# Query projections moved between the row products of a hybrid decoder kernel

## What is computed

```
qb = rmsnorm(h @ W_q), kb = rmsnorm(h @ W_k)          # 8 heads, forgetting attention (branch B)
# branch C: matrix memory, 4 heads, per head and chunk
dmat  = b_t - b_s + i_s  (s <= t)
m_t   = max(max_s dmat, b + m)
num   = (exp(dmat - m_t) * (q k^T)) @ v + exp(b + m - m_t) * C q
den   = the same with ones in place of v, and n in place of C
h     = num / max(|den|, exp(-m_t))
C_new = decay * C + sum_s w_s v_s k_s^T               # of the prompt and of each sample
```

## Time and profile before

| quantity | value |
|---|---|
| median of three runs | 3294.8 us (3291.88 to 3295.17) |
| the profiled execution | 3302.38 us, span 3300.7 us |
| PE busy | 3135.0 us, 95% of the span |
| DVE, ACT busy | 1154.3 us (35%), 818.5 us (25%) |
| mean granted TensorE clock | 0.97 |
| memory stage, from the transposes to the vb projection, layer 1 | 663.33 to 805.34 us |
| the same, layer 2 | 2298.47 to 2437.31 us |

### The profile page before, as it was taken

The page is one execution under the profiler, slowest core; times in us unless marked ns, Lnnn a source line. Parts: engine busy times, 40 slices in busy tenths (PEclk is TensorE's granted clock), DMA queues, the critical chain, the costliest instruction groups (busy, mean ns, idle before and its releaser), DMA issues.

```text
span 3300.7 us, 54135 instructions
## 1 busy us (share of the span) xinstructions
PE 3135.0 (95%) x23518; PEld 2799.6 (85%) x23518; DVE 1154.3 (35%) x1933; ACT 818.5 (25%) x1213; POOL 138.5 (4%) x269
## 2 busy tenths in 40 slices
PE   6999999989999998999989999999899999899998
PEld 4999997857677898999989999887576778899998
DVE  3333334234432234332343323332444223343333
ACT  3221224222331122211222212242223212222121
POOL 0000000000311000000000000000003120000000
PEclk9999999988999999999999999999899999999999
DMA  5444431101248432342223443312012583322212
GB/s 237 147 167 165 154 134 68 65 26 60 76 152 267 138 135 77 122 159 103 90 77 128 160 173 144 126 53 90 26 47 88 179 270 105 127 77 84 96 68 76
DMA packets 117725, 390.82 MB, mean 118 GB/s; under 512 B 12672, under 2 KB 63200, under 8 KB 99184
## 3 DMA queue, kind: packets, MB, share of 16 engines
q1 hardware_dynamic: 99456, 338.36, 29.0%
q0 software_dynamic: 14432, 34.09, 3.0%
q10 hardware_dynamic: 3600, 14.91, 1.1%
HBM read 373.62 MB, written 13.69 MB: 117 GB/s over the span
## 4 chain that ended last, share of the span: by engine, by line
PE 84%; DMA 6%; DVE 5%; ACT 3%; issue 1%; SPq 1%; ACTq 0%; DVEq 0%
PE g L838 74%; PE tb L838 5%; PE q L838 5%; DMA w<-in_w_up 3%; DMA area<-in_w_ada 1%; ACT area L1723 1%; DMA area<-in_cache_v 1%; DVE w_lo L1923 1%; DVE area L2127 1%; SPq L703 1%; ACT area L1729 0%; ACT w_hi L1460 0%; DMA area<-in_cache_k 0%; DVE w_rest L1881 0%; DVE acts_lo L1942 0%
## 5 line engine op out<-in xcount | busy, mean ns | idle before, releaser
L838 PE MATMUL g<-h_hi,w_hi 128*128 128x272 f32 x2784 | 584.4, 291 | 28.8 <-DVE h_lo L1867 12.4
L1460 ACT ACTIVATE w_hi<-w 128x1024 fp32r<-128x1024 f32 (+2 forms) x232 | 266.2, 1147 | 1271.5 <-PE g L838 930.5
L838 PE MATMUL g<-h_hi,w_lo 128*128 128x272 f32 x2784 | 579.1, 289 | 0.0
L838 PE MATMUL g<-h_lo,w_hi 128*128 128x272 f32 x2784 | 575.9, 288 | 0.0
L1923 DVE TENSOR_TENSOR w_lo<-w,w_hi 128x1024 fp32r<-128x1024 f32 (+2 forms) x232 | 309.8, 1335 | 527.1 <-ACT w_hi L1460 523.9
L838 PEld LDWEIGHTS g<-h_hi,w_hi 128*128 128x128 f32 x2784 | 440.5, 190 | 48.2 <-ACT area L1469 33.8
L838 PEld LDWEIGHTS g<-h_lo,w_hi 128*128 128x128 f32 x2784 | 439.0, 189 | 0.0
L838 PEld LDWEIGHTS g<-h_hi,w_lo 128*128 128x128 f32 x2784 | 438.2, 189 | 0.0
L838 PE MATMUL g<-h_hi,w_rest 128*128 128x272 f32 x1184 | 344.0, 293 | 0.0
L838 PE MATMUL g<-acts_hi,w_hi 128*128 128x272 f32 x1408 | 294.8, 290 | 0.0
L838 PE MATMUL g<-acts_hi,w_lo 128*128 128x272 f32 x1408 | 291.2, 288 | 0.0
(11 more groups left out here) (296 smaller groups left out, 4142.8 us busy)
## 6 DMA issues: line engine op xcount, KB each, us to landing
w<-in_w_up SPq DMA_DIRECT2D x44, 2048.0 KB, 8.1
w<-in_w_ada SPq DMA_DIRECT2D x32, 2048.0 KB, 8.2
w<-in_w_in SPq DMA_DIRECT2D x16, 2048.0 KB, 8.3
w<-in_w_down SPq DMA_DIRECT2D x16, 1536.0 KB, 7.2
w<-in_w_gate SPq DMA_DIRECT2D x48, 512.0 KB, 5.7
w<-in_w_down SPq DMA_DIRECT2D x16, 1280.0 KB, 5.7
area<-in_cache_k SPq DMA_DIRECT2D x72, 256.0 KB, 4.1
area<-in_cache_v SPq DMA_DIRECT2D x72, 256.0 KB, 4.6
```

Of the source, the lines that this page charges most:

```text
L838: return pe.matmul(o, a, b, start=start, stop=stop, skip_group_check=True, **kw)
L1460: ac.activation(WH[i % 2][:, 0:n], W[place][:, o:o + n], ACT.Copy).then_inc(s_wh, 1)
```

## The change

The schedule gets four ticks ahead of the heads: six blocks behind each of the four row products. The 16 steps of the heads hold 4 blocks (12 steps) and 5 (the last four) in place of 5 each, the five ticks of the tail 8, 8, 8, 6, 6 in place of 12, 12, 8, 8, 8. All later ticks are renumbered by HEADS_AT = 4. ScalarE and VectorE get the reads and splits that belong to the new ticks, ScalarE between its GB copies, VectorE ahead of the copy of the sample rows.

```
-IN_MLSTM = Schedule(0, FILL_A, [5] * 16 + [12, 12, 8, 8, 8])
+ROWS_AT, HEADS_AT = 0, HC
+IN_MLSTM = Schedule(0, FILL_A, [6] * HC + [4] * 12 + [5] * 4 + [8, 8, 8, 6, 6])
 ...
                 for h in range(HC):
                     product(unit(), [sel_neg[:, HB + h, :]], lambda k: ROWG[0:ROWS, :])
+                    fill(l, IN_MLSTM, ROWS_AT + h)
 ...
-                each(4, lambda i, p: ac.activation(halves(GB[:, i, :]), both(p), ACT.Copy))
+                for h in range(HC):
+                    read(l, IN_MLSTM.early[ROWS_AT + h])
+                    p = mine()
+                    drained(ac.activation(halves(GB[:, h, :]), both(p), ACT.Copy), p)
+                    read(l, IN_MLSTM.late[ROWS_AT + h])
 ...
                 un.take(4)
+                for h in range(HC):
+                    lo_fills(l, IN_MLSTM.early[ROWS_AT + h] + IN_MLSTM.late[ROWS_AT + h])
```

In the two state products of the samples, the order of the four products changes, and the wait for the spread v of both heads stands ahead of the first:

```
                     p = unit()
-                    for h2 in range(2):
-                        wait(t["vblk"])
-                        h = 2 * hp + h2
-                        for sh in range(2):
+                    wait(t["vblk"], 2)
+                    for sh in range(2):
+                        for h2 in range(2):
+                            h = 2 * hp + h2
                             last = mm(G[64 * h2:64 * h2 + 64, 2 * p + sh, :], KCT[0:NS, TILES, h * 64:(h + 1) * 64],
                                       VBLK[0:NS, h2, 4 * sh:4 * sh + 4, :], True, True)
```

More of the change, by code:

```diff
@@ L1145, in _ @@
                             qk(n + 1)
-                        fill(l, IN_MLSTM, n)
+                        fill(l, IN_MLSTM, HEADS_AT + n)
                         weigh(n)
@@ L1168, in _ @@
                 last.then_inc(s_sintra, 1)
-                fill(l, IN_MLSTM, 16)
+                fill(l, IN_MLSTM, HEADS_AT + 16)
                 wait(t["sw"])
@@ L1183, in _ @@
                 last.then_inc(s_num, 1)
-                fill(l, IN_MLSTM, 17)
+                fill(l, IN_MLSTM, HEADS_AT + 17)
                 wait(t["kws"])
@@ L1194, in _ @@
                     last.then_inc(s_unit, 1)
-                    fill(l, IN_MLSTM, 18 + hp)
+                    fill(l, IN_MLSTM, HEADS_AT + 18 + hp)
                 p = unit()
@@ L1200, in _ @@
                 last.then_inc(s_unit, 1)
-                fill(l, IN_MLSTM, 20)
+                fill(l, IN_MLSTM, HEADS_AT + 20)
                 project_tokens(l, "vb", sums=True)
@@ L1634, in _ @@
                         n = h * TILES + j
-                        read(l, IN_MLSTM.early[n])
+                        read(l, IN_MLSTM.early[HEADS_AT + n])
                         a = COL[:, j * 12 + HB + h:j * 12 + HB + h + 1]
@@ L1644, in _ @@
                         last.then_inc(s_e, 1)
-                        read(l, IN_MLSTM.late[n])
+                        read(l, IN_MLSTM.late[HEADS_AT + n])
                     un.take()
@@ L1649, in _ @@
                 un.take()
-                read(l, IN_MLSTM.early[16] + IN_MLSTM.late[16])
+                read(l, IN_MLSTM.early[HEADS_AT + 16] + IN_MLSTM.late[HEADS_AT + 16])
                 wait(t["stn"])
@@ L1660, in _ @@
                 last.then_inc(s_ses, 1)
-                read(l, IN_MLSTM.early[17] + IN_MLSTM.late[17])
+                read(l, IN_MLSTM.early[HEADS_AT + 17] + IN_MLSTM.late[HEADS_AT + 17])
                 ac.wait_ge(s_outa, outs.value())
@@ L1664, in _ @@
                     un.take()
-                    read(l, IN_MLSTM.early[18 + hp] + IN_MLSTM.late[18 + hp])
+                    read(l, IN_MLSTM.early[HEADS_AT + 18 + hp] + IN_MLSTM.late[HEADS_AT + 18 + hp])
                     if hp == 1:
@@ L1670, in _ @@
                 un.take()
-                read(l, IN_MLSTM.early[20] + IN_MLSTM.late[20])
+                read(l, IN_MLSTM.early[HEADS_AT + 20] + IN_MLSTM.late[HEADS_AT + 20])
                 wait(t["stn"])
@@ L1674, in _ @@
                 wait(t["yc"])
-                read(l, IN_MLSTM.early[21] + IN_MLSTM.late[21])
+                read(l, IN_MLSTM.early[HEADS_AT + 21] + IN_MLSTM.late[HEADS_AT + 21])
                 ac.wait_ge(s_outa, outs.value())
@@ L2115, in _ @@
                             diag(n + 1)
-                        lo_fills(l, IN_MLSTM.early[n])
+                        lo_fills(l, IN_MLSTM.early[HEADS_AT + n])
                         wait(t["e"])
@@ L2120, in _ @@
                                          ALU.mult).then_inc(s_wt, 1)
-                        lo_fills(l, IN_MLSTM.late[n])
+                        lo_fills(l, IN_MLSTM.late[HEADS_AT + n])
                     p = mine()
@@ L2135, in _ @@
                 ve.sem_inc(s_stn, 1)
-                lo_fills(l, IN_MLSTM.early[16] + IN_MLSTM.late[16])
+                lo_fills(l, IN_MLSTM.early[HEADS_AT + 16] + IN_MLSTM.late[HEADS_AT + 16])
                 ve.tensor_tensor(ARG[0:NS], GB[0:NS, :, NP:T], seq_later[:, None, :].to_broadcast([NS, HC, NS]),
@@ L2157, in _ @@
                 last.then_inc(s_sw, 1)
-                lo_fills(l, IN_MLSTM.early[17] + IN_MLSTM.late[17])
+                lo_fills(l, IN_MLSTM.early[HEADS_AT + 17] + IN_MLSTM.late[HEADS_AT + 17])
                 wait(t["num"])
@@ L2175, in _ @@
                     p = mine()
-                    lo_fills(l, IN_MLSTM.early[18 + hp] + IN_MLSTM.late[18 + hp])
+                    lo_fills(l, IN_MLSTM.early[HEADS_AT + 18 + hp] + IN_MLSTM.late[HEADS_AT + 18 + hp])
                     ve.tensor_tensor(CS[:, hp].rearrange("p (a s) v -> p a (s v)", a=2),
@@ L2187, in _ @@
                 ve.sem_inc(s_stn, 1)
-                lo_fills(l, IN_MLSTM.early[20] + IN_MLSTM.late[20] + IN_MLSTM.early[21])
+                lo_fills(l, IN_MLSTM.early[HEADS_AT + 20] + IN_MLSTM.late[HEADS_AT + 20] + IN_MLSTM.early[HEADS_AT + 21])
                 lo_part(l, *[("vb", i) for i in range(4)], ("merge", 0))
```

## The result

| kernel | median, runs | ratio to before, 95% |
|---|---|---|
| before | 3294.99 us (3291.88 to 3298.64), 4 | |
| after | 3316.74 us (3315.91 to 3317.99), 4 | 1.0068 [1.0053, 1.0083] |

The change costs 21.7 us. The forecast of 3299 us had the sign but a fifth of the size, and the range ended at 3309: the prediction was wrong. The profiled execution took 3317.99 us (span 3316.3).

A forecast was written before the change was run, and what follows sets the result against it. TensorE bounds the kernel, carrying 84% of the chain of waits. Row stage 5.1, heads -2.9, tail 0 give 2.2 us per layer, 4.4 in both: 3302.4 to 3306.8 us profiled, 3299 us as median, range 3290 to 3309.

The forecast's parts named there:

- the sign: Whole kernel: the change makes it slower, by 2.2 us per layer, 4.4 in both.
- row stage, work and wait, less the 15.86 of before: Row stage: 17.3 us of work at full clock, 0.9 for switches and 0.8 of added wait, against 15.86 now.
- row stage, clock: Row stage: blocks bring the clock back within a tick or two; 4 us at the lower clock, 2.0 lost.
- heads, blocks and ends: Heads: blocks save 3.4 and 0.3 us, first end 1.1 longer, third 0.3 shorter; -2.9 us per layer.
- heads, clock: Heads: lower-clock stretches after each boundary (0.73 and 0.88) left as they are, so no change.
- tail: Tail: twelve blocks less, but new waits; taken as 0, between -2.1 and +1.6 us per layer.
- The range of none to 6: Row stage: ends of the clock loss, none to 6 us, around the 2.0 taken.
- the three ends: Heads, last weighing to next head's first: 10.2 us at the first boundary, 8.9 at the others.
- the two added waits: TensorE waits 0.8 us at the first weighing and idles some 2.7 us for a weight block's rest in the tail.
- the alternation at nothing: State products: alternating two heads costs nothing, as two already run at a time; 1.9 us as before.
- The first rival: Row stage: row products hold the clock down, 4 us more per layer, num another 1.6; 3310 us, chance 0.33.
- The second, heads that get warmer: Heads: blocks leave them warmer, one 4.4 us stretch goes per layer, all else at low end; 3282 us, chance 0.13.

The follow-up runs named there:

- e3: Kernel after with 28 products nobody reads added ahead of the wait for the rows, before the row stage; 3311.51 us, ratio 1.0054.
- e4: Kernel after with 36 products nobody reads added at each of the three ends of heads, ahead of the next head's first blocks; 3287.61 us, ratio 0.9982.
- e6: Kernel before with 36 products nobody reads added at each of the same three ends of heads; 3277.30 us, ratio 0.9953.
- e12: Kernel after with five blocks for six behind each row product, the four left over in the tail's first tick; 3289.52 us, ratio 0.9978.
- e2: Kernel after with the state products in their old order, so the schedule change alone; 3313.89 us, ratio 1.0062.
- e8: Kernel after with one block moved from the tail to the heads' last step; 3303.91 us, ratio 1.0036.
- e5: Kernel after with unread products added: 28 ahead of the rows, 36 at each of three ends of heads, 24 in the tail; 3283.90 us, ratio 0.9967.
- e7: Kernel before with unread products added: 28 ahead of the rows and 36 at each of three ends of heads; 3273.71 us, ratio 0.9939.
- e9: Kernel before with another table: heads 5, 5, 5, 5, then three times 12, 4, 4, 4 blocks, tail 12, 8, 8, 4, 4; 3258.47 us, ratio 0.9887.

## Why the prediction was wrong, by its steps

| step, per layer | forecast | layer 1, 2 | what the runs show |
|---|---|---|---|
| row stage, work and wait, less the 15.86 of before | +3.1 | +4.5 | 20.35 at clock 1.00 (e3), 19.0 forecast |
| row stage, clock | +2.0 | +2.5, +5.5 | the stage less 20.35 |
| heads, blocks and ends | -2.9 | -2.1 | e4 against e6 at clock 1.00 |
| heads, clock | 0 | +2.1, +4.1 | low clock's cost after less before |
| tail | 0 | +0.3, +1.8 | its upper end, 1.6, with num at 6.83 us |
| sum | +2.2 | +7.3, +13.8 | |

**The step that failed** is the sentence on the heads: "the stretches at the lower clock after each boundary (clock 0.73 and 0.88) I leave as they are." I had forecast the ends to the tenth of a microsecond, the first one 1.1 us longer, and had read what stands behind an end in rows 5, and did not join the two. Those stretches were worth 8 to 10 us per layer before anything was changed, the largest thing to be won in the stage, and they grew by 3.1 us on average, more than the 2.1 us that the blocks gave: 6.2 of the 16.6 us that the forecast's sum missed in both layers. What it lacked was the link from the idle time to the clock behind it, which e4, e6 and e12 show.

**The clock of the row stage** was the second miss: 4.0 us on average for 2.0. One execution gives this value only roughly: the four kernels that have this stage with the idle ahead left alone (after, e2, e4, e8) show eight of them, from 21.88 to 25.82 us, 23.5 on average, a loss of 3.2. With the idle filled (e3, e5) the four stages take 20.35 to 20.92. My reason, blocks from 1.3 us on bring the clock back, is true, but the start differs: the same stage with the same 3.46 us of idle ahead ran at 0.88 and 0.77 in the two layers, and that of e12, with four blocks less, at 0.63 in layer 1. The range of none to 6 held these; the value did not.

**The work of the row stage** was 1.4 us short. I took half of a row product's 1.81 us for full clock. In e5, whose stage in layer 1 is at 1.00, a tick with its row product takes 3.54 us, from one product's start to the next:

```profile
662.08 1.16 PE L839 MATMUL g<-area,cst 12*128 12x272 f32 x4
...
665.62 1.18 PE L839 MATMUL g<-area,cst 12*128 12x272 f32 x4
```

With six blocks at 0.376 (2.26) that leaves 1.28 us for the product and both switches, for my 0.91 and 0.1 to 0.2: four times 0.2 to 0.3. The 0.91 was right (in e7 a row product at full clock starts at 659.91 and the next at 660.83), so the switches cost more than I gave them. The sample rows with the first head's row product took 1.56 us in the kernel after (678.49 to 680.05) for my 1.2.

**Right** were the sign, the three ends, the two added waits (the four terms of the first one add up to 4.2 us, not 4.1), the alternation at nothing, and that the tail gives nothing for its twelve blocks. The first rival (3310 us) was on the side on which the result fell. Its condition, 8 us at the lower clock in the row stage, was met in layer 2 (0.77 over 25.82 us is 12 us) and not in layer 1 (0.88 over 22.83 us is 5.5 us), but its mechanism is not borne out for the changed stage: with the idle ahead filled, the same row products between the ticks left the clock up (e3, e5). The second, heads that get warmer, had it the wrong way round here, though the mechanism is real: e12, four blocks away, is 27 us faster than the kernel after.

**Open** stays what sets how long the lower clock lasts at the start of the row stage from one layer, kernel and execution to the next (with the same idle ahead, 0.77 to 0.92 over the stage in after, e2, e4 and e8), and how the tail of e9 divides.

## What to carry to other kernels

Price an idle time of the engine that bounds the kernel twice: once as it is, and once by the lower clock of the stretch that follows it, read from the stretch behind every such gap; in e12 the second part was twice the first. Work that can be moved belongs first into the gaps that it can close (an end of a head holds twelve blocks), not into a stage where the engine never waits. And where a table deals out work in periods, see whether its period puts a helper's long operation ahead of the one wait that counts each time: five blocks for six behind each of four products, with the four left over in the tail, moved 27 us.

## What the runs showed that I had not expected

- Work without use pays: 36 products in each of three ends, 4.3 us each, made the kernel after 29 us faster and the one before 16.4 us.
- The length of the idle alone does not tell the clock behind it: after 4.26 us the next stretch ran at 0.88 before the change, after 4.25 us at 0.72 in the kernel after.
- Row products of 12 rows in a run let the clock fall 2.0 and 5.0 us into the stage even when TensorE was busy up to its start (e7), while the same products with blocks between them kept 1.00 through all four ticks (e3, e5).
